# Scan mixer: set-up made in the feed-forward stage before it, and its 32 steps spread from slot 6 on

## What is computed

```python
x = first_block(x, ...)     # per layer: top-k attention beside a state-space mixer, then a
                            # feed-forward with a causal convolution
return second_block(x, ...) # per layer: the lines below

h = rms_norm_2(x, norm1_g[l]); z = h @ w_in[l]
(cq, ckv, kpe, gq, gk, gv, glr, gr, su, gates) = split_in(z)
o_a = mla_mixer(cq, ckv, kpe, ...)       # 8 heads, softmax attention
o_b = gla_mixer(gq, gk, gv, glr, gr, ...)  # gated linear attention, chunks of 64
o_c = s5_mixer(su, lam_re, lam_im, b_re, b_im, c_re, c_im, d, log_dt, w_glu, b_glu)
merged = g0 * (o_a @ w_br_mla) + g1 * (o_b @ w_br_gla) + g2 * (o_c @ w_br_s5)
x = x + merged @ w_out[l]
h2 = rms_norm_2(x, norm2_g[l])
x = x + square(relu(h2 @ w_ff1[l])) @ w_ff2[l]
```

```python
step = exp(log_dt)
lam_bar = exp(lam * step)                            # lam complex
b_bar = ((lam_bar - 1) / lam) * (b_re + 1j * b_im)
bu = einsum(u, b_bar)                                # complex, per token
states[t] = lam_bar * states[t-1] + bu[t]            # 32 groups x 64 states
y = real(states) c_re - imag(states) c_im + d * u
y = gelu(y); y = y * sigmoid(y @ w_glu + b_glu)
```

## Time and profile before

| | |
|---|---|
| median of three runs | 2554.58 us |
| the profiled execution | 2549.25 us, span 2547.2 us |
| TensorE matmul busy | 2392.8 us, 94% of the span |
| VectorE busy | 1771.5 us, 70% |
| ScalarE busy | 1362.0 us, 53% |
| POOL busy | 262.0 us, 10% |
| granted TensorE clock, mean | 0.952 |
| HBM read | 391.93 MB, 154 GB/s |

### The profile page before, as it was taken

One profiled execution on the slowest core, in us unless ns is written; L12 is line 12 of the kernel. 1 busy time (PEld: TensorE's weight loads), 2 busy tenths in 40 slices (PEclk: granted clock), 3 DMA queues, 4 the chain that ended last, 5 costly groups with the idle time before them and its releaser, 6 DMA issues.

```text
span 2547.2 us, 43618 instructions
## 1 busy us (share of the span) xinstructions
PE 2392.8 (94%) x17968; PEld 2233.8 (88%) x17968; DVE 1771.5 (70%) x3151; ACT 1362.0 (53%) x2140; POOL 262.0 (10%) x308
## 2 busy tenths in 40 slices
PE   3999999999999999999999898998999898998999
PEld 2988899999988898999999796788999796788999
DVE  5885767578669677675674948886654948976653
ACT  3566886466447578754654416454544416454543
POOL 0000000022000000000210313300000413300000
PEclk9999999999999999999999869999999959999999
DMA  7543446557745444564654413343554312244553
GB/s 278 173 152 120 163 166 220 191 187 229 228 155 169 135 153 158 189 216 149 185 180 151 132 38 98 100 134 124 190 183 158 125 46 96 94 133 133 179 186 124
DMA packets 110853, 395.80 MB, mean 155 GB/s; under 512 B 12320, under 2 KB 13888, under 8 KB 110400
## 3 DMA queue, kind: packets, MB, share of 16 engines
q1 hardware_dynamic: 96768, 343.52, 41.8%
q0 software_dynamic: 12160, 44.08, 5.3%
q10 hardware_dynamic: 1728, 5.43, 0.6%
HBM read 391.93 MB, written 1.05 MB: 154 GB/s over the span
## 4 chain that ended last, share of the span: by engine, by line
PE 77%; DVE 15%; ACT 3%; POOL 2%; issue 2%; DMA 1%; SPq 0%; DVEq 0%; ACTq 0%
PE bank L525 77%; DVE WL L1359 3%; ACT scr L932 1%; DMA ring<-in_w 1%; DVE arena L1423 1%; ACT L923 1%; POOL arena L2032 1%; DVE scr L1406 1%; PE bank L596 1%; POOL arena L2034 0%; POOL arena L2036 0%; DVE arena L1527 0%; DVE scr L1526 0%; DVE scr L1589 0%; DVE arena L1957 0%
## 5 line engine op out<-in xcount | busy, mean ns | idle before, releaser
L932 ACT ACTIVATE WH<-ring 128x1024 fp32r<-128x1024 f32 (+1 forms) x638 | 670.0, 1051 | 985.6 <-PE bank L525 960.5
L525 PE MATMUL bank<-HTH,WH 128*128 128x256 f32 x3392 | 998.8, 294 | 42.7 <-DVE HTL L1399 14.9
L525 PE MATMUL bank<-HTL,WH 128*128 128x256 f32 x3392 | 975.1, 287 | 0.0
L525 PE MATMUL bank<-HTH,WL 128*128 128x256 f32 x3392 | 974.5, 287 | 0.0
L1359 DVE TENSOR_TENSOR WL<-ring,WH 128x1024 fp32r<-128x1024 f32 (+2 forms) x616 | 746.5, 1220 | 213.1 <-ACT WH L932 211.7
L525 PEld LDWEIGHTS bank<-HTH,WH 128*128 128x128 f32 x3392 | 665.5, 196 | 76.3 <-issue 53.4
L525 PEld LDWEIGHTS bank<-HTL,WH 128*128 128x128 f32 x3392 | 667.2, 197 | 2.0 <-issue 1.4
L525 PEld LDWEIGHTS bank<-HTH,WL 128*128 128x128 f32 x3392 | 666.3, 196 | 0.0
L923 ACT ACT_TABLE_LOAD x114 | 146.3, 1283 | 48.0 <-PE bank L525 21.9
L525 PE MATMUL bank<-scr,cst 128*128 128x256 f32 (+2 forms) x304 | 96.6, 446 | 53.7 <-ACT scr L932 53.5
L525 PE MATMUL bank<-ff2h,WH 128*128 128x256 f32 x512 | 145.4, 284 | 0.0
(11 more groups left out here) (274 smaller groups left out, 4077.6 us busy)
## 6 DMA issues: line engine op xcount, KB each, us to landing
ring<-in_w SPq DMA_DIRECT2D x620, 512.0 KB, 3.7
arena<-in_wada POOLq DMA_DIRECT2D x80, 512.0 KB, 4.8
ring<-in_w SPq DMA_DIRECT2D x16, 384.0 KB, 3.6
arena<-in_wada SPq DMA_DIRECT2D x8, 512.0 KB, 19.5
arena<-in_wada ACTq DMA_DIRECT2D x8, 512.0 KB, 22.0
ring<-in_w SPq DMA_DIRECT2D x8, 288.0 KB, 2.8
arena<-in_s POOLq DMA_DIRECT2D x4, 512.0 KB, 3.9
cst<-in_cst SPq DMA_DIRECT2D x1, 1025.0 KB, 6.3
```

The costliest lines, as they stand in the source:

```text
L525: ins = e.matmul(out, a, b, start=(start and i == 0), stop=(stop and i == len(pairs) - 1))
L932: return e.activation(out, a, func, **kw)
```

## The change

1. The eight set-up steps become a generator of their own, `s5set`. It runs in the feed-forward stage before the mixer stage: slots 48, 50, ... 62 of `stage_b` (68 units) for the first layer, 38, 40, ... 52 of `stage_d` (64 units) for the second. Its scratch is `scr` 0 to 2 instead of `scr` 4 to 6 (`L.s`). ScalarE's first step also waits for that stage's norm.
2. POOL loads `SC5`, `SB5` and the gate weights at slot 36 of that stage. `turns` is called twice: for pairs 0 and 1 one slot before the mixer stage (in POOL's program; it waits for `tf` alone), for pairs 2 to 7 at the stage's start behind the norm and two memsets, as before.
3. The 32 scan steps go to slots 6, 7, 9, 10, 12, 14, 15, 17, 18, 20, ... 55 (1.6 slots apart, before 1.5), the last five to 57 to 61.
4. POOL's product tile `SG` moves into the cosine table of the first block, which nothing reads any more; the arena keeps an unused place of the same size.

```diff
@@ C_TICKS
-    "s5": [1, 2, 3, 4, 5, 6, 7, 8] + turn_ticks(11, 32, 3, 2) + [59, 60, 61, 62, 63],
+    "s5": turn_ticks(6, 32, 8, 5) + [57, 58, 59, 60, 61],
 }
+S5_TICKS = {stage_b: [48, 50, 52, 54, 56, 58, 60, 62], stage_d: [38, 40, 42, 44, 46, 48, 50, 52]}
@@ program
+        SG = trig[:, 0, :].rearrange("p (a b) -> p a b", b=16)
...
+        for l in range(2):
+            st = 3 + 2 * l
+            for s in S5_TICKS[STAGES[st][0]]:
+                agenda.setdefault(plan.base[st] + s, []).append(("s5set", l))
@@ tensor_program
             def s5(l):
                 L = LC
-                for i in range(8):
-                    yield
@@ scalar_program
-            def s5(l):
+            def s5set(l):
                 L = LC
                 step, r, th, tm, cs, sn, cr, ci, u1, re = (s5c(i) for i in range(10))
-                p.wait_ge(in_cols("in"))
+                p.wait_ge(in_cols("in"), h_ready(3 + 2 * l, 7))
@@ vector_program
-            def s5(l):
+            def s5set(l):
...
-                w0, w1, w2 = (t.rearrange("p (a b) -> p a b", b=32) for t in L.s)
+                w0, w1, w2 = (scr[:, i, :].rearrange("p (a b) -> p a b", b=32) for i in range(3))
...
-                m0, m1 = (L.s[0][:, 256 * i:256 * i + 256].rearrange("p (a b) -> p a b", b=16) for i in range(2))
+                m0, m1 = (scr[:, 0, 256 * i:256 * i + 256].rearrange("p (a b) -> p a b", b=16) for i in range(2))
@@ gpsimd_program
-            def turns(l):
+            def turns(l, qs):
...
-                for q in range(8):
+                for q in qs:
...
                 for l in range(2):
-                    if u == plan.base[4 + 2 * l]:
-                        p.wait_ge(h_ready(4 + 2 * l, 7))
+                    if u == plan.base[3 + 2 * l] + 36:
+                        p.wait_ge(h_ready(3 + 2 * l, 7))
                         e.dma_start(flat(SC5), io["s5"][l, 0]).then_inc(s5_in.inc(by=16), 16)
                         e.dma_start(flat(SB5), io["s5"][l, 1]).then_inc(s5_in.inc(l, by=16), 16)
                         e.dma_start(wgate, io["wgate"][l]).then_inc(wgate_in.inc(l, by=16), 16)
+                    if u == plan.base[4 + 2 * l] - 1:
+                        turns(l, (0, 1))
+                    if u == plan.base[4 + 2 * l]:
+                        p.wait_ge(h_ready(4 + 2 * l, 7))
                         e.memset(AT.rearrange("p a b c -> p (a b c)"), 0.0).then_inc(LA.G.inc(), 1)
                         e.memset(SF.rearrange("p a b c -> p (a b c)"), 0.0).then_inc(LA.G.inc("zero", l), 1)
-                        turns(l)
+                        turns(l, range(2, 8))
```

More of the change, by code:

```diff
@@ L424, in program @@
         SU, TF, CT = ar(a2["SU"], 4, T), ar(a2["TF"], 4, 256), ar(a2["CT"], 2, 2, 512)
-        SC5, SB5, SX, SG = ar(a2["SC5"], 2, 512), ar(a2["SB5"], 2, 512), ar(a2["SX"], 512), ar(a2["SG"], 16, 16)
+        SC5, SB5, SX = ar(a2["SC5"], 2, 512), ar(a2["SB5"], 2, 512), ar(a2["SX"], 512)
+        SG = trig[:, 0, :].rearrange("p (a b) -> p a b", b=16)
         MG, GX, G2 = ar(a2["MG"], 8, T), ar(a2["GX"], 8, T), ar(a2["QH"], 8, T)
@@ L877, in tensor_program @@
                     "heads0": lambda l: heads(l, 0), "heads1": lambda l: heads(l, 1), "cutm": lambda l: empty(1),
-                    "s5": s5}
+                    "s5": s5, "s5set": lambda l: empty(8)}
             live = {}
@@ L1282, in s5 @@
                     yield
+            def s5(l):
+                L = LC
                 def tanh(cc):
@@ L1308, in scalar_program @@
                     "gate3": lambda l: gate(l, 3), "cuto": cuto, "gla": gla, "norms": norms,
-                    "heads0": lambda l: heads(l, 0), "heads1": lambda l: heads(l, 1), "cutm": cutm, "s5": s5}
+                    "heads0": lambda l: heads(l, 0), "heads1": lambda l: heads(l, 1), "cutm": cutm, "s5": s5,
+                    "s5set": s5set}
             e.dma_start(cols[:, :], io["cols"]).then_inc(in_cols.inc("in", by=16), 16)
@@ L1883, in s5 @@
                             yield
+            def s5(l):
+                L = LC
+                V, r = L.V, s5c(1)
                 sets = [(L.s[0], L.s[1], L.b[0]), (L.s[2], SX, L.b[1])]
```

## The result

The changed kernel takes 2485.37 us (median of 4 runs, 2483.16 to 2489.97); the kernel before took 2553.98 us beside it (4 runs, 2551.29 to 2554.94). The ratio is 0.9735, 95% interval 0.9718 to 0.9752: 68.6 us faster. The forecast was 2494 us, range 2471 to 2538, "faster" at 0.91. The profiled execution of after is its slowest run: 2489.97 us, span 2487.9 us; the sum of the prediction had said 2489 for a profiled one.

What follows compares the result with a forecast made beforehand. TensorE, busy for 94% of the span, was taken as the bound, through its gaps and low clock. Terms: -70.2 + 0.5 + 5 + 1.3 + 3.2 = -60.2 us; profiled 2549.25 becomes 2489, plus 5.3 for the median: 2494, range 2471 to 2538.

Steps and rivals of the forecast that it cites:

- Steps 1 to 3: Scan-mixer stage before the value units: early gaps, low clock and slot 12's gap shrink, gaining 7.3, 4.2, 1.7 us per layer.
- step 6: First scan-mixer norm: POOL's rotation tables run beside it and slow VectorE's two-operand operations, +5 us (0 to 6.2).
- Step 4: Value units, slots 15 to 18: entered at full clock they keep it, gaining 21.9 us per layer.
- trap: Value units entered at the low clock (1.2 GHz) are run at it to their end; 21.9 us per layer.
- steps 1 and 2: Set-up leaves slots 1 to 8, closing early gaps (7.3 us per layer); low clock after the 4.72 us gap goes (4.2).
- the trap stays: Rival: slot 12's gap stays nearer 3.5 us and the clock falls before unit 15; 2538 us, chance 0.17.
- Step 5: Last slots of the feed-forward stages: VectorE's idle time hides the moved set-up, +0.5 us (bounds 0 and 41).
- Step 7: Second scan-mixer norm: ScalarE, left on the sine table, pays a table load there, +1.3 us.
- Step 8: Heads' stretch: new scan slots ease VectorE's load after slot 33 but three outputs wait; +3.2 us for both layers.

Runs made afterwards that it cites:

- e4: Changed kernel, with POOL making the first layer's first two rotation tables behind the mixer stage's norm, not beside it: 2479.18 us.
- e5: Changed kernel with the scan steps back at the slots of before, set-up still moved out: 2494.73 us (four executions, 2478.41 to 2504.43).
- e9: e5's kernel plus two maxima (1.4 us) of filler on VectorE in slot 12 of both mixer stages: 2530.56 us.
- e12: e8's kernel with the scan steps at the slots of before, except the first two in slots 8 and 10: 2470.23 us.
- e1: Kernel before, with only its second scan step moved from slot 12 to slot 13, set-up left in place: 2505.79 us.
- e2: Changed kernel plus 3.5 us of filler on VectorE at the end of slot 12 in both mixer stages: 2542.24 us.
- e10: Changed kernel plus two maxima (1.4 us) of filler on VectorE in slot 12 of both mixer stages: 2533.87 us.
- e3: Changed kernel plus the same 3.5 us of VectorE filler in slot 19, behind the value units, in both mixer stages: 2491.62 us.
- e11: e8's kernel with the first eight scan steps at the changed kernel's slots, the other 24 from slot 18 at 1.5 slots: 2466.90 us.
- e6: Changed kernel with the scan steps from slot 6 on at the old distance of 1.5 slots: 2481.62 us.
- e7: Changed kernel plus a small exponential ending the set-up, bringing ScalarE's table back inside the feed-forward stage: 2482.19 us.
- e8: Changed kernel with the edits of e4 and e7 together: 2480.50 us.

## Why the prediction was right, step by step

**Steps 1 to 3** (set-up out, low clock after it, slot 12; -13.2 us per layer) end at the first value unit. Measured there: -5.8 in the first layer and -8.9 in the second, with step 6 inside in the first, and with two more groups of four scan-input matmuls and one output (2 x 1.13 + 1.06 = 3.3 us) ahead of the mark than before. Taken off (3.4 for the tables by e4; the 3.3), the steps come to -12.5 and -12.2. Right, within 1 us a layer. Two things differ from the working. The two short gaps came out at 0.39 and 0.36 us where 0.6 and 1.2 were forecast. And a gap of 1.64 us before 1445 us was on no list: TensorE waits for a bank until VectorE has copied the attention's position keys out of it (L1490, one copy of 2.29 us), and rotations back of the scan now stand ahead of that copy. All nine profiled kernels with the first steps at after's slots have this gap; e5, e9 and e12, with later first steps, don't.

**Step 4** (trap, -21.9) is the right mechanism and 3 us too small. The cleanest measure is e5's profiled execution, with the scan steps at the slots of before: value section 26.1 for 49.4 us, the stretch behind it 19.1 for 20.9, 25.1 per layer. The sum had charged 192 matmuls and two pairs of inputs; the low stretch of before also ran over cuts, an output and the units behind. (After's own 27.2 hold some of the scan work that now stands in front.) e1, e2, e9 and e10, with e3 as the control, show the cause: the time follows the entry into the value units, wherever the delay comes from. Since e1 gives 47 us with the set-up in its place, the set-up's own cost (steps 1 and 2) is the smaller part. One word of the mechanism is too strong: "run at it to their end" holds for seven of the eight value sections behind a long gap (two each in before, e2, e9 and e10), but not for e10's second; and they need not be entered at the low clock, as e10's first matmul and e1's and e12's fourth units show.

**The rival "the trap stays"** was nearer than its 0.17 looks. The prediction took 0.6 + 1.2 us of gaps to be harmless, from gaps in slots 7 to 10. e10 has 0.40 and 1.81 and is in the trap. With the forecast 1.2 us before the value units, between e5's 0.88 and e10's 1.81, the outcome would have been open; that the gap came out at 0.36 us made the forecast safe. Waits before wide units do not tell what a wait before value units does.

**Step 5** (feed-forward tails, +0.5): right; from the first matmul of that feed-forward stage to the norm's sums it is +0.7 us (196.85 for 196.14). TensorE is busy for 50.00 of 50.00 and 48.00 of 48.00 us; VectorE's 42.91 and 40.16 us stand against the forecast 42.4 and 42.9.

**Step 6** (POOL beside the first norm, +5): right in place and kind. VectorE in the first norm of after:

```profile
1401.25 0.83 DVE L1407 TENSOR_TENSOR HTL<-scr,HTH 128x256 fp32r<-128x256 f32 x1
1402.01 0.83 DVE L1414 SCALAR_TENSOR_TENSOR scr<-XT,cols,scr 128x256 f32<-128x256 f32 x1
1402.77 0.95 DVE L1407 TENSOR_TENSOR HTL<-scr,HTH 128x256 fp32r<-128x256 f32 x1
```

POOL is busy for 20.49 of the 22.60 us there. Measured by undoing it: 3.4 us up to the value units, of which 2.6 are waits inside the norm (5.38 + 0.56 + 0.51 + 0.20 us for 4.03). The first chunk's delay reaches TensorE whole (5.38 for 4.03); behind it the waits are half a microsecond or less, as TensorE has matmuls to do while VectorE makes the next chunk. The count of 16 operations did not see that.

**Step 7** (+1.3): right; TensorE's gap there is 4.03 us for 2.75, and the stretch between the mixer stages is 1.3 us longer. ScalarE in the second norm of after, where the earlier trace rows read the bank straight away:

```profile
1945.38 1.28 ACT L927 ACT_TABLE_LOAD   x1 [0.88 <-PE bank L531]
1946.67 0.47 ACT L936 ACTIVATE scr<-bank,cst 128x256 f32<-128x256 f32 x1
```

**Step 8** (+3.2 for both, bounds -15 and +10 a layer): the size of the right order, the mechanism wrong. From the native units on, after is 3.5 us longer than before in the first layer and 2.3 shorter in the second, +1.2. As it has one scan output and one group of inputs (2.2 us) per layer less to do there than before, the like-for-like cost is some 5.6 us, an estimate. The step charged waits on one-slot outputs; the rotations back have 1.1 and 1.4 us of wait left in the two layers (8.6 before), the outputs' additions (L1928) 3.3 and 4.5 (5.0 and 5.1 before). What costs is in the native units, where TensorE now waits before norm sums of the heads. ScalarE in after:

```profile
1531.10 1.06 ACT L936 ACTIVATE WH<-ring 128x1024 fp32r<-128x1024 f32 x1 [2.70 <-DMA ring<-in_w]
...
1534.87 1.13 ACT L936 ACTIVATE scr<-arena 96x512 f32<-96x512 f32 x2
```

The counterpart of the first row in before, and in e11:

```profile
1554.87 1.06 ACT L932 ACTIVATE WH<-ring 128x1024 fp32r<-128x1024 f32 x1 [2.13 <-DMA ring<-in_w]
```

```profile
1522.76 1.06 ACT L936 ACTIVATE WH<-ring 128x1024 fp32r<-128x1024 f32 x1 [1.87 <-DMA ring<-in_w]
```

TensorE in after, then in e11:

```profile
1528.45 1.96 PE L531 MATMUL bank<-scr,cst 96*96 96x512 f32 x4
1530.34 1.94 PE L531 MATMUL bank<-arena,ring 128*64 128x256 f32 x8
1536.06 3.73 PE L531 MATMUL bank<-scr,cst 96*96 96x512 f32 x4 [3.78 <-ACT scr L936]
```

```profile
1520.94 1.96 PE L531 MATMUL bank<-scr,cst 96*96 96x512 f32 x4
1522.83 1.06 PE L531 MATMUL bank<-scr,arena 128*32 128x256 f32 x8
1523.82 1.13 PE L531 MATMUL bank<-arena 32*128 32x256 f32 x4
1524.88 1.94 PE L531 MATMUL bank<-arena,ring 128*64 128x256 f32 x8
1527.71 1.96 PE L531 MATMUL bank<-scr,cst 96*96 96x512 f32 x4 [0.90 <-ACT scr L936]
```

ScalarE's high copy of a coming unit waits for the weights, and the squares that TensorE wants stand behind it in ScalarE's program. That wait isn't new: before has 2.13 and 1.73 us of it, e11 1.87 and 1.57. New is what TensorE has to do meanwhile. With steps 1.6 slots apart the scan's output and inputs come behind the norm sums that TensorE waits for; 1.5 apart (e6, e11) they stand ahead of them and take 2.05 us (1522.83 to 1524.88). In the fourteen profiled stages with after's slots (after, e2, e3, e4, e7, e8, e10) TensorE's gap is 1.1 us longer than ScalarE's wait, in the four of e6 and e11 it is 1.0 us shorter. Why ScalarE waits 2.7 to 2.8 us in after's first layer and in both of e10, and 1.5 to 2.1 us everywhere else, stays open.

The gap also takes the clock down, and for how long varies:

```profile
1535.80:1549.50 13.70, 13.44 (x27) 6.35 (x28) 10.79 (x18) 5.58 (x9) 9.55 (x12) 0.50 0.07 24
```

It is low for 13.7 us here, and for 3.4 us behind the gap of 2.89 us in the second layer. In e8 and e4, gaps of 2.9 to 3.0 us have 13.6 us of low clock behind them in one layer and 3.4 in the other: that is the difference between native units of 41 and of 46 us, and a scatter of 5 us a layer in kernels with after's slots. The new spacing costs 7.9 us in the two mixer stages against e5's profiled execution, and 13.6 us from e11 to e8.

**The sum.** That the profiled execution took 2489.97 us, with 2489 forecast, is luck in part. Step 4 gave 50.2 us for 43.8, and the stretch up to the first mixer norm took 6.1 us longer in this execution, 5.4 of them ahead of any change. The 5.3 us that were added for the median have no ground in after, whose profiled execution is its slowest. The lower end of the range doesn't follow from its own words either: no POOL cost, a gain of 6.6 us a layer in step 8 and 5 us a layer more come to 2463, not 2471. Nothing hung on it.

**The clock.** The Trainium skill ("TensorE: Matmul & The Clock Gate", What's actually happening), by which activity releases the throttle and idleness brings it back, would have the low stretch end soon after the value units begin. The traces disagree: the clock is at 0.50 with TensorE busy for 49.69 of 49.70 us (e2), and it falls without idleness in e1 and e12. The measurement decides.

## What to carry to other kernels

Look for stretches that are busy and slow: where the granted clock is 0.5 through fifty microseconds, the whole stretch can be the price of one short gap at its head, and one step moved by one slot can buy it back (e1: 47 us). Then measure how near the edge the result is, by putting a microsecond or so of filler on the late engine: a gap of 0.88 us goes with times that scatter over 26 us (e5), and one of 0.36 us loses 48 us to 1.4 us of filler (e10). When woven steps get a new spacing, ask what work is left for the engine ahead of each result that it waits for: 2 us of scan matmuls on the wrong side of the norm sums brought a gap and a low clock behind it (e8 against e11).

## What had not been expected of the hardware

- Gaps of like length have different effects. Before a unit of 256-column matmuls 1.64 us leaves the clock up (after); before 128-column value units 0.88 us leaves it up in one profiled execution (e5), and 1.81, 2.33 and 3.98 us bring it down, for the whole section or, once, all but 3.5 us of it (e10, e9, e2). The same gap of 1.8 us in the native units leaves it up in before and in e5 and is followed by 6.8 us at 0.50 in e12.
- In e10 the clock falls after the gap, not in it: 0.6 us into the value units.
- The clock can fall with no gap at all, in the fourth value unit (e1, e12: 19.50 of 19.50 and 18.50 of 18.50 us busy at 0.65 and 0.63). In e1 it does so in the first layer and not in the second. e5 spreads over 26 us and e12 over 18, where before spreads over 7.3 at most; that this too is the clock falling in some executions is inferred from their mean granted clocks.
- Beside POOL's rotation tables VectorE's scalar_tensor_tensor on two SBUF tensors takes 0.83 us (0.48 in before's norm), like tensor_tensor (0.83 for 0.42). The gated step of slot 12, also beside them, took 5.0 us before and after.
